# Rotary embedding of dilated attention: the swapped halves go to a spare PSUM bank, and VectorE reads the projection straight from PSUM

## The reference, cut to what matters

```python
def apply_rope(x, cos, sin):
    xf = x.astype(jnp.float32)
    x1, x2 = jnp.split(xf, 2, axis=-1)
    return jnp.concatenate([x1 * cos - x2 * sin, x2 * cos + x1 * sin], axis=-1).astype(x.dtype)
...
q_b = apply_rope(qkv_b[:, :, 0], cos_b[:, None], sin_b[:, None])
k_b = apply_rope(qkv_b[:, :, 1], cos_b[:, None], sin_b[:, None])
y_b = dilated_mixer(q_b, k_b, qkv_b[:, :, 2])
```

## Time and profile before

| what | value |
|---|---|
| runs of the kernel before | 2700.99 us median of 3 (2696.41 to 2701.82) |
| the profiled execution | 2695.99 us |
| its span, first to last instruction | 2694.2 us |
| mean granted TensorE clock in the span | 0.973 of full speed |
| HBM read, written | 223.12 MB, 2.10 MB |

### The profile page before, as it was taken

How to read it: one execution, slowest core, us unless ns; L and a number is a source line. 1 busy time by engine, 2 the same in 40 slices (tenths; PEclk the granted TensorE clock), 3 DMA queues, 4 the chain that set the end, 5 groups by cost and what they waited for, 6 DMA issues and landing times.

```text
span 2694.2 us, 37011 instructions
## 1 busy us (share of the span) xinstructions
PE 2556.7 (95%) x12476; PEld 2079.5 (77%) x12476; DVE 1201.9 (45%) x1626; ACT 686.3 (25%) x1293; POOL 1982.1 (74%) x1558
## 2 busy tenths in 40 slices
PE   7998999999999999999999999999998899969997
PEld 5775788878788887776788877788886678848796
DVE  6846625223322125936725322422225337560775
ACT  4434314111210013524314111210002214131341
POOL 6979462899889898979563889998988573447704
PEclk9999999999999999999999999999998899979998
DMA  4233120323232323223211223223222121102201
GB/s 154 86 110 111 78 79 26 99 84 103 89 98 94 101 90 109 83 97 119 98 63 34 90 92 97 94 95 100 93 97 77 65 86 56 40 31 90 79 17 63
DMA packets 67715, 226.73 MB, mean 84 GB/s; under 512 B 7569, under 2 KB 16273, under 8 KB 66833
## 3 DMA queue, kind: packets, MB, share of 16 engines
q1 hardware_dynamic: 66736, 223.95, 25.1%
q10 hardware_dynamic: 864, 1.30, 0.1%
HBM read 223.12 MB, written 2.10 MB: 84 GB/s over the span
## 4 chain that ended last, share of the span: by engine, by line
PE 72%; POOL 11%; issue 8%; DVE 6%; DMA 2%; ACT 0%; POOLq 0%; DVEq 0%; SPq 0%; ACTq 0%
PE ps L556 17%; PE ps L558 17%; PE ps L557 17%; POOL whi L460 6%; POOL wlo L463 4%; PE ps L806 4%; PE ps L634 3%; PE ps L800 2%; PE ps L756 2%; PE ps L846 1%; PE ps L851 1%; POOL lnsq L487 1%; PE ps L749 1%; DVE q_parts L1736 1%; DMA raw<-w_gate 1%
## 5 line engine op out<-in xcount | busy, mean ns | idle before, releaser
L460 POOL TENSOR_TENSOR whi<-raw,one 128x512 fp32r<-128x512 f32 (+2 forms) x720 | 798.5, 1109 | 576.1 <-PE ps L558 532.0
L463 POOL TENSOR_TENSOR wlo<-raw,whi 128x512 fp32r<-128x512 f32 (+2 forms) x720 | 948.7, 1318 | 56.4
L556 PE MATMUL ps<-h,whi 128*128 128x512 f32 x1984 | 796.9, 402 | 44.2 <-POOL wlo L463 18.9
L557 PE MATMUL ps<-h,whi 128*128 128x512 f32 x1984 | 781.7, 394 | 0.0
L558 PE MATMUL ps<-h,wlo 128*128 128x512 f32 x1984 | 781.3, 394 | 0.0
L556 PEld LDWEIGHTS ps<-h,whi 128*128 128x128 f32 x1984 | 376.8, 190 | 146.2 <-issue 30.3
L558 PEld LDWEIGHTS ps<-h,wlo 128*128 128x128 f32 x1984 | 376.6, 190 | 81.7
L557 PEld LDWEIGHTS ps<-h,whi 128*128 128x128 f32 x1984 | 377.5, 190 | 78.6 <-issue 2.4
L556 PE MATMUL ps<-y,whi 128*128 128x512 f32 x640 | 250.3, 391 | 0.6 <-DVE y L1660 0.6
L557 PE MATMUL ps<-y,whi 128*128 128x512 f32 x640 | 249.3, 389 | 0.0
L558 PE MATMUL ps<-y,wlo 128*128 128x512 f32 x640 | 249.2, 389 | 0.0
(11 more groups left out here) (247 smaller groups left out, 3261.4 us busy)
## 6 DMA issues: line engine op xcount, KB each, us to landing
raw<-w SPq DMA_DIRECT2D x120, 512.0 KB, 3.2
raw<-w_abc SPq DMA_DIRECT2D x68, 512.0 KB, 3.3
raw<-w_ada SPq DMA_DIRECT2D x48, 512.0 KB, 3.3
raw<-w_gate SPq DMA_DIRECT2D x48, 512.0 KB, 3.3
raw<-w_in SPq DMA_DIRECT2D x44, 512.0 KB, 3.3
raw<-w_pac SPq DMA_DIRECT2D x16, 512.0 KB, 3.2
raw<-w_o SPq DMA_DIRECT2D x16, 512.0 KB, 3.2
raw<-w_out SPq DMA_DIRECT2D x16, 512.0 KB, 3.3
```

The costliest lines, as they stand in the source:

```text
L460: pool.tensor_tensor(whi[:, s, r], raw[:, s, r], one[:, 0:1].to_broadcast([P, cols // 2]), ALU.mult).then_inc(hi_made, 1)
L463: pool.tensor_tensor(wlo[:, s, r], raw[:, s, r], whi[:, s, r].bitcast(F32), ALU.subtract).then_inc(made, 1)
L556: nc.tensor.matmul(out, whi[:, s, w], moving[:, c, :], start=(c == 0), stop=False)
L557: nc.tensor.matmul(out, whi[:, s, w], rest[:, c, :], start=False, stop=False)
```

## The change

ACT no longer copies the unit to SBUF. It writes the four exchanged pieces to PSUM bank 4 + s and raises a new semaphore, `swapped[s]`; it no longer raises `bank_free[s]`. DVE waits for `swapped[s]`, multiplies bank s by the cosine table (and by the scale of the queries) into `tmp[s]` in SBUF, and that operation raises `bank_free[s]`. Then it multiplies bank 4 + s by the sine table in place, waits for both of its own operations (`bank_free[s]` and the new `half_turned`), and adds bank 4 + s and `tmp[s]` into `qb` or `kb`. The order of the units, PE's and POOL's programs and all DMAs are the same; `b_rest` and `lead` stand where they stood.

```diff
-STEPS_1 = (2 + 3 + 2 + 2 * B_TILES + 2 + 6 + NQB * (B_HEADS + 1) + A_HEADS + NQB + NQB * (C_HEADS + 1) + DC
+STEPS_1 = (2 + 3 + 2 + 2 + 6 + NQB * (B_HEADS + 1) + A_HEADS + NQB + NQB * (C_HEADS + 1) + DC
...
+        swapped = [sem(f"swapped{s}") for s in range(2)]
+        half_turned = sem("half_turned")
...
                         for s in range(2):
                             act.wait_ge(fin_done, fin_n.next())
                             act.wait_ge(unit_done[s], ud_n[s].next())
-                            nc.scalar.activation(prob[:, s, 0:T], ps[s][:], ACT.Copy, scale=scale)
                             for half in range(4):
                                 to, frm = 32 * half, 32 * (half ^ 1)
-                                last = nc.scalar.activation(tmp[s][to:to + 32, :], ps[s][frm:frm + 32, :], ACT.Copy,
+                                last = nc.scalar.activation(ps[4 + s][to:to + 32, :], ps[s][frm:frm + 32, :], ACT.Copy,
                                                             scale=scale)
-                            last.then_inc(bank_free[s], 1)
+                            last.then_inc(swapped[s], 1)
...
-                def b_rope(dst, first, times):
-                    with repeat(dve, times, [(free_n[0], 1), (free_n[1], 1), (st_n, 2)]) as j:
+                def b_rope(dst, first, times, scale=1.0):
+                    with repeat(dve, times, [(free_n[0], 1), (free_n[1], 1), (swap_n[0], 1), (swap_n[1], 1),
+                                             (turned_n, 2)]) as j:
                         for s in range(2):
+                            dve.wait_ge(swapped[s], swap_n[s].next())
+                            nc.vector.scalar_tensor_tensor(out=tmp[s], in0=ps[s][:], scalar=scale, in1=rope[:, 0, :],
+                                                           op0=ALU.mult, op1=ALU.mult).then_inc(bank_free[s], 1)
+                            nc.vector.tensor_tensor(ps[4 + s][:], ps[4 + s][:], rope[:, 1, :], ALU.mult).then_inc(half_turned, 1)
                             dve.wait_ge(bank_free[s], free_n[s].next())
-                            t = prob[:, s, 0:T]
-                            nc.vector.tensor_tensor(tmp[s], tmp[s], rope[:, 1, :], ALU.mult)
-                            step(nc.vector.tensor_tensor(t, t, rope[:, 0, :], ALU.mult))
+                            dve.wait_ge(half_turned, turned_n.next())
                             to = dst[:, bass.ds(2 * j + (first + s), 1), :].rearrange("p a (f i) -> p (a i) f", f=4)
-                            nc.vector.tensor_tensor(to, t.rearrange("p (i f) -> p i f", f=4),
+                            nc.vector.tensor_tensor(to, ps[4 + s][:].rearrange("p (i f) -> p i f", f=4),
                                                     tmp[s].rearrange("p (i f) -> p i f", f=4),
                                                     ALU.add).then_inc(fin_done, 1)
...
-                b_rope(qb_, 0, 3)
+                b_rope(qb_, 0, 3, HD_SCALE)
```

More of the change, by code:

```diff
@@ L1335, in _ @@
             sig_n, mhi_n, mg_n, pr_n, ir_n, si_n = Count(), Count(), Count(), Count(3), Count(), Count()
+            swap_n, turned_n = [Count(), Count()], Count()
             qb_n, odd_n, mix_n, y2hi_n, qhi_n, bl_n = Count(), Count(), Count(), Count(), Count(), Count()
@@ L1444, in _ @@
             with repeat(dve, DEPTH, [(st_n, STEPS_1), (ud_n[0], 75), (ud_n[1], 75), (free_n[0], 59), (free_n[1], 59),
-                                     (nsum_n, 3), (std_n, 3), (rsb_n, 4), (hhi_n, 2 * DC), (post_n, 10), (rb_n, 3), (ir_n, 16),
+                                     (nsum_n, 3), (std_n, 3), (rsb_n, 4), (hhi_n, 2 * DC), (post_n, 10), (rb_n, 3), (swap_n[0], 6), (swap_n[1], 6), (turned_n, 12), (ir_n, 16),
                                      (nope_n, A_HEADS), (bl_n, 2), (s_n, 80), (t_n, 80), (o_n, 12), (yhi_n, 12), (bias_n, 3),
```

## The result

The changed kernel is slower: ratio 1.004 to the kernel before, 95% interval 1.0022 to 1.0059, from ten runs of each (medians 2710.70 and 2696.88 us). The profiled execution took 2704.31 us with a span of 2702.5, 8.3 us more than before's. On the base of 2696.88 the ratio is +10.8 us (5.9 to 15.9); the prediction said +12.5. (The difference of the two medians, 13.8 us, lies in the same interval.) The base of the forecast, 2700.99 from three runs, was 4.1 us above the median of ten, so only the difference is compared. One of the 23 executions of the kernel before that the experiments were compared with took 3739.4 us at a granted clock of 0.643, and the ratios leave it out.

The account below looks back on a forecast made before the run. TensorE was taken to bound the kernel, with GpSimd not holding it. New standing of 15.9 us less 8.7 old gave +7.2, clock falls 5.3: +12.5 on 2701.0, so 2713.5 us, range 2703 to 2722.

Parts of the forecast that it names:

- The bound: In the rotated-unit stage of each layer, TensorE at its pace plus bank waits, not GpSimd; 0.2 us waited for GpSimd.
- The most that could be given back: TensorE's waits behind late rotations, 8.7 us, and one clock fall, 2.65 us: at most 11.4 us.
- Operations: VectorE's three rotation operations with one PSUM input: 0.69 us each, 2.3 us per unit in place of 4.9.
- (a): Before each layer's third unit, TensorE waits for VectorE's first multiply: 4.3 and 4.2 us, together 8.5 us.
- (b): Behind b_rest of q, the first multiply of k releases bank 0 late: 0.9 us per layer, 1.8 us in all.
- rival 2: b_rest shrinks because GpSimd idles when it starts: no change, +3.3 us, 2704.3 us; chance 0.13.
- (c): Behind b_rest of k, after the tenth unit, TensorE waits for the bank: 2.8 us per layer, 5.6 us in all.
- Clock: Falls of TensorE's clock behind the new waits: three in place of one, 2.65 us each, 5.3 us more.
- The sum: Whole kernel: standing +7.2 us and clock falls 5.3 us, total +12.5 us, giving 2713.5 us.
- The range's lower end: 2703 us for the whole kernel, taking uncontended b_rests with no extra clock fall but one.
- The first: GpSimd was the stage's true bound, so all 11.4 us come back: faster, 2689.6 us; chance 0.04.
- The third: PSUM operands bring no relief in the rotations, or writing PSUM is dear: slower still, 2722 us; chance 0.08.

Follow-up runs that it names:

- four banks: Kernel before with its twelve rotated units going round four PSUM banks instead of two: ratio 1.0015, median 2704.16 us.
- the kernel with the later split: Changed kernel with the split of the keys (lead, memsets, b_rest) after the last two rotated units instead of before them: ratio 1.0016, median 2701.89 us.
- the one with plain order: Changed kernel whose last rotation operation writes the tokens in plain order instead of grouped by phase: one run, 2704.00 us.
- the kernel with the release alone: Kernel before, still SBUF to SBUF, with bank_free raised by VectorE's first rotation multiply instead of ScalarE's last piece: ratio 1.0127, median 2731.93 us.

## Why the prediction was right, by its own steps

- **The bound.** Right: PE, held by a bank and not by POOL, in the kernel before. But the prediction took the table's 0.2 us of waiting for POOL as a sign of slack, and there was next to none. The kernel before stands at two limits at once, 0.4 us apart at most: with the bank's waits gone, POOL's take their place (84.20 for 84.16 and 84.55).
- **The most that could be given back, 11.4 us.** Slightly small: the stage's floor is 77.17 us, so 14.4 us were there in two layers. The prediction counted waits and one fall, and left out the 0.3 us that each restart of PE costs and the small waits of the weight loads.
- **Operations.** First and second operation: 0.69 us, measured 0.691 and 0.689 in the median. The write to PSUM cost DVE nothing here, and ACT's pieces became shorter, 0.564 for 0.589 us. Third: sized at 0.69, measured 1.106 for its strided output; it lies behind the release, so the sum wasn't touched.
- **The page's rule against the change.** The Trainium skill, VectorE: DVE Perf Modes, in the section on the TRN2 errata, has 62 cycles more for a PSUM source. The 0.691 us here, against 0.68 for SBUF in the earlier trace rows, don't show it; the trace decides.
- **(a), 8.5 us.** Right: 3.99 and 3.98 us by PE's timeline. From start to start it is 44.85 - (39.80 + 0.81) = 4.24 us, where the 0.81 is what lay between the spread and the third unit before, 39.11 to 39.92; 4.3 and 4.2 were said.
- **(b), 0.9 each.** Measured 0.50 and 0.42. b_rest took 5.33 us in place of 6.12; that is rival 2's mechanism (a POOL that isn't saturated when b_rest begins), and about half of this term went and nothing of the next.
- **(c), 2.8 each.** Measured 3.04 twice; b_rest of the keys 5.49 us.
- **Clock.** Three falls in place of one, 2.65 each, were said. There were two of 2.28, both at (a). At (c) it fell in neither layer of this trace, but in one of the two layers in two of the experiments; two falls in six waits would make 2.7 falls in the mean, and nearer to three than this trace shows. This term was the most oversized: two falls of 2.28 in place of one of 2.65 are +1.9 us, where +5.3 was said. Standing is +6.2 us (14.9 less 8.7), where +7.2 was said.
- **The sum.** The stage grew by 7.1 us in the pair of traces, and 12.5 was said; the measured 10.8 us lie between. The ten runs spread from 2700.35 to 2717.63 us, and the profiled one was among the faster. The mechanism is shown, but what makes 10.8 out of 7.1 is in no trace, so it is partly luck that the number came so near. The range's lower end doesn't follow from its own terms either: uncontended b_rests with one more fall are rival 2's 2704.3, not 2703.
- **Rivals.** The first, that POOL was the true bound and all would come back, is wrong for the kernel before as it stands and right for it with four banks, where PE waits for line 463 as the rival said. The rule that it leant on, the shared port pair of the Trainium skill's SBUF — State Buffer (SBUF: two separate sides), agrees with the trace: POOL's pairs went from 1.47 + 1.90 to the uncontended 1.04 + 1.29 beside rotations with an operand in PSUM. The second, that b_rest shrinks, came in part at (b) and not at (c). The third fell with the durations.

## What to carry to other kernels

Before moving a buffer's release to another engine, write down what stands ahead of it in that engine's queue at every place where the producer will ask, the first iteration above all: here 30 us less work on VectorE per layer bought nothing, and three waits that sum to 7.5 us per layer made the kernel slower. When a wait table names one releaser with large waits and another with 0.2 us, the second may be just behind; free both, or expect the one to take the other's place. Where PSUM has idle banks, a longer round lets a release be late: it took the changed kernel from 1.004 to 0.9956. By itself, on the kernel before, it gained nothing (1.0015).

## What the runs showed of the hardware that was not expected

- A VectorE addition whose output goes to SBUF in steps of 512 bytes took 1.106 us, in plain order 0.692 (128x512 fp32). The Trainium skill, SBUF — State Buffer, in the section Door 1: The DMA port swizzle, tells of 16-byte lines in SBUF and a penalty for leaving one at each access; the two durations agree with that.
- ScalarE's 32x512 piece from PSUM took 589 ns into SBUF and 564 ns into PSUM.
- The granted clock fell to 1.2 GHz behind every wait of PE of 3.98 us or more in this stage: two each in the changed kernel, the kernel with the later split and the one with plain order, six in the kernel with the release alone. Behind the waits of 3.04 and 3.05 us it fell in two of six, and behind the kernel before's 2.80 and 2.82 us in the second alone. What tells these apart wasn't tried.
